# Two heads at a time in both attentions of a two-block program, and three parts put in another order

## The reference

```python
# block 1, per block of 128 queries: top-k search, then attention over latents
q      = einsum('btr,rhd->bthd', cq, w_uq)                 # 8 heads of 64
q_abs  = einsum('bthd,hcd->bthc', q, w_uk) * 64 ** -0.5    # absorbed: 128 wide
_, sel = lax.top_k(score, 256)                             # keys kept per query
logits = einsum('bthc,btkc->bthk', qa, ckv[sel]) + bias    # -inf where rel < 0
o      = einsum('bthk,btkc->bthc', softmax(logits), ckv[sel])
y_att  = einsum('bthc,hcd->bthd', o, w_uv)                 # back to 64 per head
# block 1, decays: y_rwkv = rwkv7_scan(r, decay, k, v, -kk, kk * a), normed and gated
mix    = concatenate([y_att, y_rwkv]) @ w_out              # then norm, FFN, norm
# block 2: u = rmsnorm(h); q_lat, kv_lat, k_rope and others = u @ w_in
q, kv  = rmsnorm(q_lat) @ w_q_up, rmsnorm(kv_lat) @ w_kv_up  # 8 heads: 64 + 32 rope; 64 + 64
pr     = softmax(where(k_chunk <= q_chunk, q k^T * 96 ** -0.5, min))
ob     = pr @ v                                            # then w_b_out, gates, w_o, FFN, ...
```

## Time and profile before

| | us |
|---|---|
| median of 3 runs | 3829.42 (3828.99 to 3829.85) |
| the profiled execution | 3827.32 |
| its span, first to last instruction | 3826.0 |
| mean granted TensorE clock | 0.952 of full speed |

### The profile page before, as it was taken

The page is one execution under the profiler, slowest core; times in us unless marked ns, Lnnn a source line. Parts: engine busy times, 40 slices in busy tenths (PEclk is TensorE's granted clock), DMA queues, the critical chain, the costliest instruction groups (busy, mean ns, idle before and its releaser), DMA issues.

```text
span 3826.0 us, 51800 instructions
## 1 busy us (share of the span) xinstructions
PE 3473.7 (91%) x21830; PEld 2725.6 (71%) x21846; DVE 1779.5 (47%) x2886; ACT 917.6 (24%) x1666; POOL 345.7 (9%) x277
## 2 busy tenths in 40 slices
PE   6989658887889899999997898999999999999998
PEld 3757447674667688888885676886667788887877
DVE  2258886653335622223453444532226544444556
ACT  2146523332332500000122233100004211111112
POOL 0000156661000000000000000000000000000000
PEclk8999778998999999999999999999999999999999
DMA  6156301110011311112231100111124111113434
GB/s 202 43 67 209 127 18 52 36 41 12 17 56 61 116 55 48 47 50 83 94 132 57 34 1 23 50 28 50 37 90 132 55 50 45 50 45 115 143 105 149
DMA packets 216071, 270.22 MB, mean 71 GB/s; under 512 B 11068, under 2 KB 176226, under 8 KB 215587
## 3 DMA queue, kind: packets, MB, share of 16 engines
q1 hardware_dynamic: 210555, 247.87, 20.3%
q10 hardware_dynamic: 3192, 11.17, 1.6%
q0 software_dynamic: 2096, 7.87, 0.5%
HBM read 232.80 MB, written 34.08 MB: 70 GB/s over the span
## 4 chain that ended last, share of the span: by engine, by line
PE 75%; DVE 8%; ACT 3%; issue 2%; POOL 0%; DMA 0%; DVEq 0%; ACTq 0%; POOLq 0%
PE psum L1934 17%; PE psum L1936 17%; PE psum L1938 17%; PE psum L2951 3%; PE psum L1174 3%; PE psum L1706 2%; PE psum L1729 2%; PE psum L2800 2%; PE psum L2448 2%; PE psum L2654 2%; PE psum L2822 2%; PE psum L2811 1%; PE psum L1717 1%; PE psum L1192 1%; PE psum L1760 0%
## 5 line engine op out<-in xcount | busy, mean ns | idle before, releaser
L1934 PE MATMUL psum<-hT_hi,wcut_lo 128*128 128x512 f32 x1856 | 588.9, 394 | 16.8 <-DVE hT_lo L1973 16.8
L1938 PE MATMUL psum<-hT_lo,wcut_hi 128*128 128x512 f32 x1856 | 582.0, 390 | 0.0
L1936 PE MATMUL psum<-hT_hi,wcut_hi 128*128 128x512 f32 x1856 | 581.9, 390 | 0.0
L1934 PEld LDWEIGHTS psum<-hT_hi,wcut_lo 128*128 128x128 f32 x1856 | 350.0, 189 | 96.7 <-DVE hT_lo L1973 17.9
L1938 PEld LDWEIGHTS psum<-hT_lo,wcut_hi 128*128 128x128 f32 x1856 | 349.8, 188 | 73.4
L1936 PEld LDWEIGHTS psum<-hT_hi,wcut_hi 128*128 128x128 f32 x1856 | 350.1, 189 | 72.7
L1916 DVE CAST wcut_hi<-raw 128x1024 fp32r<-128x1024 f32 x256 | 176.9, 691 | 475.0 <-PE psum L1938 450.5
L1934 PE MATMUL psum<-wcut_hi,xcut_lo 128*128 128x512 f32 x1120 | 348.1, 392 | 19.0 <-DVE xcut_lo L2052 13.8
L1936 PE MATMUL psum<-wcut_hi,xcut_hi 128*128 128x512 f32 x1120 | 346.7, 391 | 0.0
L1938 PE MATMUL psum<-wcut_lo,xcut_hi 128*128 128x512 f32 x1120 | 346.5, 391 | 0.0
L1033 POOL TENSOR_TENSOR st<-st,nhalf 128x1 f32<-128x1 f32 (+2 forms) x78 | 62.0, 802 | 3046.3 <-DVE st L674 3046.3
(11 more groups left out here) (434 smaller groups left out, 4629.8 us busy)
## 6 DMA issues: line engine op xcount, KB each, us to landing
raw<-in_w_ffn_down SPq DMA_DIRECT2D x88, 512.0 KB, 3.5
raw<-in_w_ffn_up SPq DMA_DIRECT2D x66, 512.0 KB, 3.8
slot<-in_ada_w SPq DMA_DIRECT2D x24, 1024.0 KB, 11.4
raw<-in_w_in SPq DMA_DIRECT2D x28, 512.0 KB, 5.4
raw<-in_w_ffn_gate SPq DMA_DIRECT2D x22, 512.0 KB, 3.8
slot<-in_w_in SPq DMA_DIRECT2D x8, 1024.0 KB, 6.0
raw<-in_w_out SPq DMA_DIRECT2D x16, 512.0 KB, 3.5
x_one<-xrow SPq DMA_DIRECT2D x16, 512.0 KB, 2.7
```

What stands on the lines that cost most here:

```text
L1934: pe.matmul(outs[i], al, bs[i][0], start=start, stop=False, skip_group_check=True)
L1936: pe.matmul(outs[i], ah, bs[i][0], start=False, stop=False, skip_group_check=True)
L1938: mm = pe.matmul(outs[i], ah, bs[i][1], start=False, stop=stop, skip_group_check=True)
```

## The change

*First attention.* 32 rounds of (pair of heads q, tile t), the tiles in the order 4, 3, 5, 2, 6, 1, 7, 0. Queries and keys are now projected per pair into 64 rows for each head (`query_tensor`; kT from ckvT2 by wuk), values once for all heads (`values_tensor`, Va). The scores of the two heads alternate on the two row halves of the array and take all four score banks in one round. DVE divides the weights by their sum in place (`normed_vector`) before PE turns them. The outputs of the pair go to the two column halves, values loaded and weights moving, and come out turned already, in one bank for one copy into mixT. wukT, oT, ya and the transposes at the end go. Four distance buffers in place of two; SP's row loads of x stand behind the end of the attention.

*Second attention.* 16 rounds per half of (tile, pair), the same scheme, the scores of the heads one after the other; all copies of turned weights are ACT's; outputs straight into obT.

*Decays.* The search's steps stand behind a round's tile work, two per round up to round 20 and then one, up to round 29. Pe before mx on DVE, PC before the Square on ACT.

*Latents.* Outputs of p2's tiles 0 to 3 interleaved with the tail, L2448 waits tile by tile, position copy ahead of q's norm, the second norm of k behind the qlT scaling.

```diff
+def best_steps(g):
+    return 2 if g < 21 else 1
...
     if j == 2:
+        v.wait_ge(*S.at(("Pi", t)))
+        v.scalar_tensor_tensor(Pe, sig, 0.5 * E05, bank(K, 7), MUL, ADD).then_inc(*V.up(("Pe", t)))
         v.wait_ge(*G.at(("mixed", t)))
         v.tensor_tensor(mx, mx, K.prev[:, 0:1024], ADD).then_inc(*V.up(("mx", t)))
-        v.wait_ge(*S.at(("Pi", t)))
-        v.scalar_tensor_tensor(Pe, sig, 0.5 * E05, bank(K, 7), MUL, ADD).then_inc(*V.up(("Pe", t)))
...
         s.activation(K.Pes[t % 3], K.Pes[t % 3], ACT.Exp, bias=K.mask("shift")[:, 2:3]).then_inc(*S.up(("Pe", t)))
+        s.wait_ge(*T.at(("tot", t)))
+        s.activation(K.PCs[:, t % 4, :], p[:, 0:8], ACT.Exp, bias=K.mask("shift")[:, 3:4]).then_inc(*S.up(("PC", t)))
...
         s.wait_ge(*V.at(("kk", t)))
         s.activation(K.tmp, K.kk, ACT.Square).then_inc(*S.up(("kk", t)))
-        s.wait_ge(*T.at(("tot", t)))
-        s.activation(K.PCs[:, t % 4, :], p[:, 0:8], ACT.Exp, bias=K.mask("shift")[:, 3:4]).then_inc(*S.up(("PC", t)))
...
 def rwkv_tensor(pe, K):
-    rwkv_start(pe, K)
...
     for g, tiles in rounds_of():
-        if g < BEST_ROUNDS:
-            for _ in range(3):
-                next(K.best, None)
...
+        if g < BEST_ROUNDS:
+            for _ in range(best_steps(g)):
+                next(K.best, None)
...
-ATT = [(h, t) for h in range(8) for t in range(NT)]
+ORDER = (4, 3, 5, 2, 6, 1, 7, 0)
+ATT = [(q, t) for q in range(4) for t in ORDER]
...
+    fence(sp, K, "att")
     for t in range(4):
         post_load(sp, K, K.posts["p1"], t)
...
+def scores_tensor(pe, K, r):
...
+    for b in range(4):
+        pe.wait_ge(*B.free(b))
+    for o in range(0, W, 512):
+        n = min(512, W - o)
+        for par in range(2):
+            d = slice(64 * par, 64 * par + 64)
+            mm = pe.matmul(bank(K, 2 * par, 2)[:, o:o + n], K.qT1[q % 2][d, t * 128:(t + 1) * 128], K.kT1[q % 2][d, o:o + n], start=True,
+                           stop=t < 2, skip_group_check=True)
...
+def turned_tensor(pe, K, r, par):
...
+    pe.wait_ge(*V.at(("norm", r, par)))
...
+def outputs_tensor(pe, K, r):
...
+    for b in range(t + 1):
+        for par in range(2):
+            mm = pe.matmul(bank(K, 6)[64 * par:64 * par + 64, 0:128], K.Va[:, b, (2 * q + par) * 64:(2 * q + par + 1) * 64],
+                           K.pT[2 * (r % 2) + par][:, b, :], start=b == 0, stop=b == t, skip_group_check=True)
...
 def att_tensor(pe, K):
...
+    for r in range(len(ATT) + 3):
         if 2 <= r < len(ATT) + 2:
+            turned_tensor(pe, K, r - 2, 0)
         if r < len(ATT):
+            scores_tensor(pe, K, r)
+        if 2 <= r < len(ATT) + 2:
+            turned_tensor(pe, K, r - 2, 1)
+        if r >= 3:
...
+            outputs_tensor(pe, K, r - 3)
+        if 2 <= r % 8 < 6 and r < 24:
+            query_tensor(pe, K, r // 8 + 1, r % 8 - 2, 7)
...
+def normed_vector(v, K, r):
...
+    v.wait_ge(*S.at(("exp", r, 1)))
+    v.reciprocal(K.s1[:, 3, i:i + 2], K.s1[:, 2, i:i + 2]).then_inc(*V.up())
+    v.wait_ge(*V.own())
+    for par in range(2):
+        L = K.Lg[i + par][:, 0:W]
+        v.tensor_scalar(L, L, K.s1[:, 3, i + par:i + par + 1], None, MUL).then_inc(*V.up(("norm", r, par)))
...
-def tail_vector(v, K, P):
+def tail_vector(v, K, P, outs=False):
...
             post_mean(v, K, P, n)
+            if outs:
+                post_out_vector(v, K, P, n - 4)
...
-    if t % 4 == 0:
+    if t == 0:
         pe.wait_ge(*D["w0" if key == "q" else "w1"].at(("lat2", key)))
-        for E in (V, S):
-            pe.wait_ge(*E.at(("hT", "p2", t + 3)))
+    for E in (V, S):
+        pe.wait_ge(*E.at(("hT", "p2", t)))
...
-    lat2_norm(v, K, ("q",), slice(0, 8), 0, 384, "q normed")
     v.wait_ge(*T.at("pos"))
     v.tensor_copy(K.pos, bank(K, 0)[:, 0:8]).then_inc(*V.up("pos"))
+    lat2_norm(v, K, ("q",), slice(0, 8), 0, 384, "q normed")
...
-    v.wait_ge(*S.at(("lat2", "k", 7)))
-    lat2_norm(v, K, ("k", 1), HALVES[1], 384, 256, ("k normed", 1))
     for t in range(0, NT, 2):
         v.wait_ge(*T.at(("qlT", t)))
...
+    v.wait_ge(*S.at(("lat2", "k", 7)))
+    lat2_norm(v, K, ("k", 1), HALVES[1], 384, 256, ("k normed", 1))
...
-TILES2 = [(t, h) for t in range(NT) for h in range(4)]
+ORDER2 = (3, 4, 2, 5, 1, 6, 0, 7)
+ROUNDS2 = [(t, p) for t in ORDER2 for p in range(2)]
...
+def scores2_tensor(pe, K, hh, r):
...
+    for par in range(2):
+        h, b = 2 * p + par, 2 * par
+        pe.wait_ge(*B.free(b))
+        pe.wait_ge(*B.free(b + 1))
...
+def outputs2_tensor(pe, K, hh, r):
...
+    o = 6 + r % 2
...
+            mm = pe.matmul(bank(K, o)[64 * par:64 * par + 64, 0:128], K.Vv[:, b, (2 * p + par) * 64:(2 * p + par + 1) * 64],
+                           K.pT2[2 * (r % 2) + par][:, b, :], start=b == 0, stop=b == t, skip_group_check=True)
```

More of the change, by code:

```diff
@@ L1629, in rwkv_scalar @@
     for g, tiles in rounds_of():
-        if g < BEST_ROUNDS:
-            for _ in range(3):
-                next(K.sums, None)
-        if g == BEST_ROUNDS:
-            for _ in K.sums:
-                pass
         for t, r in tiles:
@@ L1642, in rwkv_scalar @@
                 front_scalar(s, K, t, r)
+        if g < BEST_ROUNDS:
+            for _ in range(best_steps(g)):
+                next(K.sums, None)
+        if g == BEST_ROUNDS:
+            for _ in K.sums:
+                pass
 def rwkv_pool(g, K):
@@ new lines, in values_tensor @@
+def values_tensor(pe, K, t, b):
+    T, V, S, B = K.T, K.V, K.S, K.bank
+    pe.wait_ge(*B.free(b))
+    pe.matmul(bank(K, b), K.ckvT2[:, t * 128:(t + 1) * 128], K.wuv.rearrange("p a b -> p (a b)"), start=True, stop=True,
+              skip_group_check=True).then_inc(*T.up(("values", t)))
+    B.until(b, S if t % 2 else V, ("values", t))
+def scores_tensor(pe, K, r):
+    T, V, S, B = K.T, K.V, K.S, K.bank
+    q, t = ATT[r]
+    W = (t + 1) * 128
+    if t == ORDER[0]:
+        pe.wait_ge(*S.at(("query", q, 1)))
+        pe.wait_ge(*V.at(("query", q, 3)))
+    for b in range(4):
+        pe.wait_ge(*B.free(b))
+    for o in range(0, W, 512):
[4 more added lines that the diff above has]
+                           stop=t < 2, skip_group_check=True)
+            if t < 2:
+                mm.then_inc(*T.up(("qk", r, par)))
+    if t >= 2:
+        pe.wait_ge(*V.at("maskb"))
+        for par in range(2):
+            for o in range(0, W, 512):
+                n = min(512, W - o)
+                mm = pe.matmul(bank(K, 2 * par, 2)[:, o:o + n], K.idbf, K.maskb[:, MOFF[t] + o:MOFF[t] + o + n], start=False, stop=True,
+                               skip_group_check=True)
+            mm.then_inc(*T.up(("qk", r, par)))
+    for par in range(2):
+        for b in (2 * par, 2 * par + 1):
+            B.until(b, V, ("max", r, par))
@@ new lines, in turned_tensor @@
+def turned_tensor(pe, K, r, par):
+    T, V, S, B = K.T, K.V, K.S, K.bank
+    t = ATT[r][1]
+    L = K.Lg[2 * (r % 3) + par]
+    pe.wait_ge(*V.at(("norm", r, par)))
+    for g0 in range(0, t + 1, 4):
+        b = 4 + g0 // 4
+        pe.wait_ge(*B.free(b))
+        for k in range(g0, min(t + 1, g0 + 4)):
+            tr = pe.transpose(bank(K, b)[:, (k - g0) * 128:(k - g0 + 1) * 128], L[:, k * 128:(k + 1) * 128], K.ident)
+        tr.then_inc(*T.up(("turn", r, par, g0)))
+        B.until(b, S, ("pT", r, par, g0))
+    T.mark(("turn", r, par))
@@ new lines, in att_vector, with turned_scalar @@
+        if 1 <= r < len(ATT) + 1:
+            normed_vector(v, K, r - 1)
+        if 2 <= r % 8 < 6 and r < 24:
+            query_vector(v, K, r // 8 + 1, r % 8 - 2, 7)
+def turned_scalar(s, K, r, par):
+    T, S = K.T, K.S
+    t = ATT[r][1]
+    if r >= 2:
+        s.wait_ge(*T.at(("pv", r - 2)))
+    for g0 in range(0, t + 1, 4):
+        n = min(t + 1, g0 + 4) - g0
+        s.wait_ge(*T.at(("turn", r, par, g0)))
+        s.activation(K.pT[2 * (r % 2) + par][:, g0:g0 + n, :].rearrange("p a b -> p (a b)"), bank(K, 4 + g0 // 4)[:, 0:n * 128],
+                     ACT.Copy).then_inc(*S.up(("pT", r, par, g0)))
+    S.mark(("pT", r, par))
@@ new lines, in turned2_tensor @@
+def turned2_tensor(pe, K, hh, r, par):
+    T, V, S, B = K.T, K.V, K.S, K.bank
+    t = ROUNDS2[r][0]
+    L = K.Lg2[2 * (r % 3) + par]
+    pe.wait_ge(*V.at(("norm2", hh, r, par)))
+    for g0 in range(0, t + 1, 4):
+        b = 4 + g0 // 4
+        pe.wait_ge(*B.free(b))
+        for k in range(g0, min(t + 1, g0 + 4)):
+            tr = pe.transpose(bank(K, b)[:, (k - g0) * 128:(k - g0 + 1) * 128], L[:, k * 128:(k + 1) * 128], K.ident)
+        tr.then_inc(*T.up(("turn2", hh, r, par, g0)))
+        B.until(b, S, ("pT2", hh, r, par, g0))
+    T.mark(("turn2", hh, r, par))
@@ new lines, in att2_vector @@
+        for r in range(LAST2 + 5):
+            if r >= 4:
+                t, p = ROUNDS2[r - 4]
+                v.wait_ge(*T.at(("pv2", hh, r - 4)))
+                v.tensor_copy(K.obT[:, 2 * hh + p, t * 128:(t + 1) * 128], bank(K, 6 + r % 2)[:, 0:128]).then_inc(*V.up(("ob", hh, r - 4)))
+            if r <= LAST2:
```

(19 more changed lines are left out.)

470 lines of the change are left out of this document (175 added, 295 removed).

## The result

The changed kernel takes 3670.98 us (3669.98 to 3676.93, 4 runs) against 3829.2 (3826.81 to 3829.85, 4 runs). The ratio is 0.9589 with a 95% interval of 0.9574 to 0.9605, so 158 us less. The forecast was 3660, its range 3630 to 3690. The profiled execution is the longest of the four, 3676.93, with a span of 3675.6; its numbers are compared with those of the profiled execution before (3827.32).

The account below looks back on a forecast made before the run. PE was taken to bound the kernel, busy 91% of the span. Gains of 97 (first attention), 25 (second), 25 (latents) and 22 (decays) sum to 169, from 3827.3 to 3658, so a median of 3660, range 3630 to 3690.

Parts of the forecast that it names:

- First attention, 97 predicted: First attention falls from 297.1 us to 200, a gain of 97, with ends at 65 and 112.
- The price I took for the column halves: Attention outputs: a pair of heads costs 0.235 us per key block, bounded above by 0.47.
- The 200: First attention's predicted length in us, from PE's 163 or the chain's 154 + 12 plus additions; ends 185 and 230.
- The chain: First attention: maximum, reciprocals, division, transposes, scores and mask, 38.4 us per pair of heads, 154 for four pairs.
- The row halves: First attention's scores: two heads on 64 rows each cost as one, 31 us for four pairs.
- Second attention, 25 predicted: Second attention takes 81.5 us a half, gaining 2 x 12.5 = 25, range 15 to 35.
- Latents, 25 predicted: Latents and the tail before them: waits of 6.13, 12.75 and 6.09 us go, gain 25, range 17 to 28.
- Decays, 22 predicted: Decay part: fewer waits in early rounds and for PC in later ones, together 22 us, range 0 to 45.
- in sum I take 10: Decay part, early rounds: PE's waits shrink by 10 us with the search steps moved, range 0 to 25.
- of 4.4 I keep 3, four times 3 = 12: Decay part, later rounds: PC going first saves 3 us in each of four waits, 12 in all, up to 20.
- rival (b): Decay part gains nothing: search steps in rounds 17 to 29 meet full DVE work; 3682 us, chance 0.10.
- Rival (c): TensorE's granted clock stays at the lower level through both attentions, slower than before: about 3905 us, chance 0.04.

Follow-up runs that it names:

- e8: Both attentions of the changed kernel, with DVE dividing head 0's weights between the two maxima and head 1's behind them: 3669.67 us.
- e5: The changed kernel with the first attention's scores of a pair issued one head after the other instead of alternating between row halves: 3675.73 us.
- e10: The changed kernel with three search steps a round instead of two and then one, still behind the tiles' work: 3686.96 us.

## Why the prediction was right, step by step

- *First attention, 97 predicted, 100 measured.* The work of PE was right: 139 us at full clock and 24 of shape changes make 163 in my sum, and the trace has 168.0 busy of 197.0. The price I took for the column halves, 0.235 for a key block of a pair, is 0.246 in the trace (eight such blocks, 32 records, in 1.97 us). The 200 was luck in part. It is 163 + 8 + 7 + 12 + 5 + 5, and the 12 for the first queries and values is in the 163 already, against what stands in brackets there. Without it PE's side comes to 188 and the chain's to 191. Nor is 185 what is left if none of the additions is due; that is 163 or 166.
- *The chain.* It was named as a bound beside PE. Moving the division out of it (e8) moved the waits and not the stage, so this isn't borne out. What stands beside PE's work is 29 us of idle time, 20 of it in front of the transposes and shared among the division, the maximum and ACT's copies.
- *The row halves* were right in price, and the reason I gave, that the heads alternate, isn't needed (e5).
- *Second attention, 25 predicted, 28.5 measured*, with the clock at 1.00 and 0.98 where I had it at 0.95 from the kernel before.
- *Latents, 25 predicted, 24.9 measured.* The sum was right by luck, by errors that cancel. Of the waits of 12.75, 6.13 and 6.09 us the first is down to 0.77 and the last to 1.53, but the 6.13 for hTb in the middle of the tail is still there, unchanged. What made up for it: the waits in front of the two halves of q's product are gone (1.91 and 1.43 us before), the first half of that product takes 20.84 for 22.57, and k's product 31.28 for 34.12, at full clock.

```profile
1965.64 4.01 PE L2225 MATMUL psum<-ident,y 128*128 128x128 f32 x16 [6.13 <-ACT hTb L2253]
```

- *Decays, 22 predicted, none gained (6.6 lost in the profile, 1.4 to 6.6 over the seven profiles of this code).* This is the step that failed: "in sum I take 10" and "of 4.4 I keep 3, four times 3 = 12". The early rounds did save 8 us, and the same steps cost 8 in rounds 21 to 28, DVE being busy 43.4 us there for 28.9. That is rival (b), which I gave 0.10, by the mechanism that it names; the cover that I set against it, DVE busy 17.2 of 35 us, was read late in the part, from 850 to 885, and not in those rounds. PC gave 6 at most by round 49, since half of its wait comes back as the wait for Pe. The first wait of 5.72, which I had as gone, moved on by one matmul:

```profile
439.64 2.07 PE L1447 MATMUL psum<-wlo,lora 64*128 64x512 f32 x2 [5.60 <-DVE sig L1486]
```

- *The total.* In the profiled execution the 3658 of the sum, with 22 not gained and 6.6 lost, become 3686.6; the attentions gave 3.1 and 3.5 us beyond their terms and the stages at nothing 3.5, which makes 3676.5 against 3676.93. The median is 6 lower and so 11 from the forecast. The 10 us from other stages weren't foreseen, so that it came so near is luck in part.
- *Rival (c)*, the lower clock in the attentions: it was there for the start (0.66 over 887 to 907) and gone after; over the rest it is 0.94, with PE busy 157 of 183 us.

## What to carry to other kernels

Price a stage by the work of its fullest engine and by the waits that really stand in front of it, and don't trust a single chain that ends about where its neighbours do: taking the division out of it moved the waits to other instructions and left their sum at 20 us. A small operation behind a large one on the same engine (a copy of 0.16 us behind a norm of 12 us) is the cheapest thing to find in a profile and was worth 15.8 us, a quarter of it with the clock. When side work fills an engine that others wait for, look at that engine in the very rounds to which the work moves: spread over more rounds it saved 8 us early and cost 8 later, and only less of it made the part shorter.

## What the runs showed of the hardware

- Matmuls on the two row halves of TensorE overlapped without being issued in turn: 8 records took 1.78 us with one head's all ahead of the other's in the program, and 1.77 alternating. On the two column halves the order decided: 3.33 us against 1.97 for 32 records. The Trainium skill (TensorE: Matmul & The Clock Gate, "Packing small matmuls", The mechanism) has weight loads overlap only when the row group differs; here the loads of 64 columns with all 128 rows did not keep the alternating halves from running side by side, by the 1.97 us above, and the measurement decides. The same section has matmuls in program order at start and end; in e5's records 512-wide matmuls of the second head start ahead of the first head's 384-wide ones, so that it does not hold for the order in which this program was written.
- The shape change is seen in the changed kernel too. Five transposes at 0.11 are 0.55 and the scores start 0.70 after them, so 0.15 us go at the change, near the 0.19 of the earlier trace rows:

```profile
1007.22 0.77 PE L1753 MATMUL psum<-ident,Lg 128*128 128x128 f32 x5 [0.28 <-DVE Lg L1836]
1007.92 1.56 PE L1727 MATMUL psum<-kTa,qTa 64*128 64x512 f32 x8
```

- The same program's time moved by 20 us in e10 (3668.57 to 3688.52) with the mean granted clock (0.960 to 0.955). The first attention's stage moved by up to 6 us between profiles with its clock (197 at 0.93, 191 to 195 at 0.95 to 0.97), and one and the same stretch of the decays by 7 (120.9 at 0.93, 128.2 at 0.84).
